# The memory's norm gain moved from its tokens into its weights, in a fused two-block transformer kernel

## The reference

```
def rmsnorm(x, gain):
    y = x32 * lax.rsqrt(jnp.mean(x32 * x32, axis=-1, keepdims=True) + EPS)
    return (y * gain.astype(f32)).astype(x.dtype)
...
    km, vm = jnp.split(mem_n @ w_kv, 2, axis=-1)      # mem_n = rmsnorm(mem, norm_mem)
```

## Time and profile before

| | us |
|---|---|
| median of 3 runs | 756.17 (754.99 to 756.32) |
| the profiled execution, its time | 757.29 |
| its span, first to last instruction | 755.5 |
| TensorE matmuls busy | 737.4 (98%) |
| VectorE busy | 523.7 (69%) |
| ScalarE busy | 472.9 (63%) |
| DMA queue of SyncE | 125.91 MB, 52.2% of 16 engines' span |

### The profile page before, as it was taken

The page is one execution under the profiler, slowest core; times in us unless marked ns, Lnnn a source line. Parts: engine busy times, 40 slices in busy tenths (PEclk is TensorE's granted clock), DMA queues, the critical chain, the costliest instruction groups (busy, mean ns, idle before and its releaser), DMA issues.

```text
span 755.5 us, 10829 instructions
## 1 busy us (share of the span) xinstructions
PE 737.4 (98%) x3887; PEld 612.0 (81%) x3887; DVE 523.7 (69%) x811; ACT 472.9 (63%) x746; POOL 10.9 (1%) x18
## 2 busy tenths in 40 slices
PE   8999999999999999999999999998899999999998
PEld 5778888987898888888888887866679888888886
DVE  5686596676767777767547487999957765567540
ACT  6676648866367778777435776666636776557420
POOL 0004000000000000000000000000000000000000
PEclk9999999999999999999999999999999999999999
DMA  8875465434366665456656356210247755566630
GB/s 280 284 257 171 131 190 187 152 114 147 111 218 205 218 222 183 150 170 208 198 178 191 118 167 196 85 56 29 71 144 235 236 193 175 173 223 212 208 109 28
DMA packets 70986, 128.87 MB, mean 171 GB/s; under 512 B 5575, under 2 KB 17823, under 8 KB 70944
## 3 DMA queue, kind: packets, MB, share of 16 engines
q1 hardware_dynamic: 70366, 125.91, 52.2%
q10 hardware_dynamic: 578, 2.40, 1.0%
HBM read 127.24 MB, written 1.05 MB: 170 GB/s over the span
## 4 chain that ended last, share of the span: by engine, by line
PE 88%; DMA 4%; DVE 4%; ACT 2%; issue 1%; SPq 1%; DVEq 0%; ACTq 0%
PE acc L600 26%; PE acc L602 26%; PE acc L601 26%; DMA b_x<-in_x 1%; PE banks L739 1%; DMA b_raw<-in_w_in 1%; DVE b_wlo L1484 1%; PE banks L651 1%; PE banks L634 1%; PE banks L914 1%; DMA b_gain<-in_norm_ffn 1%; PE banks L621 1%; DMA b_gates<-in_b_gate 1%; PE banks L666 1%; PE banks L780 1%
## 5 line engine op out<-in xcount | busy, mean ns | idle before, releaser
L1484 DVE TENSOR_TENSOR b_wlo<-b_raw,b_whi 128x1024 fp32r<-128x1024 f32 (+3 forms) x244 | 274.3, 1154 | 89.8 <-ACT b_whi L1029 88.4
L1029 ACT ACTIVATE b_whi<-b_raw 128x1024 fp32r<-128x1024 f32 (+3 forms) x244 | 239.2, 1003 | 122.7 <-PE acc L602 45.3
L600 PE MATMUL acc<-b_whi,b_hhi 128*128 128x512 f32 (+4 forms) x528 | 201.8, 382 | 2.6 <-DVE b_wlo L1484 1.1
L602 PE MATMUL acc<-b_wlo,b_hhi 128*128 128x512 f32 (+4 forms) x528 | 196.5, 372 | 0.0
L601 PE MATMUL acc<-b_whi,b_hlo 128*128 128x512 f32 (+4 forms) x528 | 196.3, 372 | 0.0
L600 PEld LDWEIGHTS acc<-b_whi,b_hhi 128*128 128x128 f32 x528 | 99.4, 188 | 22.3 <-issue 2.8
L602 PEld LDWEIGHTS acc<-b_wlo,b_hhi 128*128 128x128 f32 x528 | 99.4, 188 | 15.3
L601 PEld LDWEIGHTS acc<-b_whi,b_hlo 128*128 128x128 f32 x528 | 99.6, 189 | 14.2
L600 PE MATMUL acc<-b_whi,b_ohi 128*128 128x512 f32 (+1 forms) x272 | 105.8, 389 | 0.3 <-DVE b_olo L2030 0.3
L602 PE MATMUL acc<-b_wlo,b_ohi 128*128 128x512 f32 (+1 forms) x272 | 103.6, 381 | 0.0
L601 PE MATMUL acc<-b_whi,b_olo 128*128 128x512 f32 (+1 forms) x272 | 103.5, 380 | 0.0
(11 more groups left out here) (258 smaller groups left out, 748.6 us busy)
## 6 DMA issues: line engine op xcount, KB each, us to landing
b_raw<-in_w_in SPq DMA_DIRECT2D x48, 512.0 KB, 4.3
b_raw<-in_w_ffn_up SPq DMA_DIRECT2D x40, 512.0 KB, 4.8
b_raw<-in_w_ffn_in SPq DMA_DIRECT2D x40, 512.0 KB, 4.6
b_raw<-in_w_ffn_down SPq DMA_DIRECT2D x22, 512.0 KB, 5.8
b_raw<-in_w_ffn_out SPq DMA_DIRECT2D x22, 512.0 KB, 4.5
b_raw<-in_w_out SPq DMA_DIRECT2D x16, 512.0 KB, 3.8
b_raw<-in_w_in SPq DMA_DIRECT2D x12, 412.0 KB, 3.6
b_raw<-in_w_in SPq DMA_DIRECT2D x8, 410.0 KB, 3.6
```

The lines of the kernel that those rows point to most:

```text
L600: nc.tensor.matmul(o, a, wh, start=first, stop=False)
L602: mm = nc.tensor.matmul(o, a, wl, start=False, stop=last)
L1029: A(whi[:, n % SPLIT, 0:c["nk"], 0:c["n"]], raw[:, n % RAW, 0:c["nk"], 0:c["n"]], ACT.Copy)\
L1484: V.tensor_tensor(wlo[:, n % SPLIT, 0:c["nk"], 0:c["n"]], raw[:, n % RAW, 0:c["nk"], 0:c["n"]], whi[:, n % SPLIT, 0:c["nk"], 0:c["n"]].bit ...
```

## The change

The gain is loaded as 8 rows of 128 entries instead of one row of 1024, and one transpose on TensorE makes of it a tile of 128 partitions x 8 columns, copied by ScalarE into `gcol`. The rounded part of the four `mkv` chunks is made with that column as the scale, the rest by a scaled subtract; each chunk takes two instructions on each engine, one for each 128 features, in place of one. The memory's tokens are turned straight from `memx` when they have landed; the four gain multiplies and the spread go. Two more idle matmuls follow the turned gain. SyncE's wait before it overwrites `memx` at group `fg0` is on the four turned banks instead of the gain multiplies. One wait is added ahead of the turn of `iq` in the second block, on a group that was finished long before. VectorE no longer waits for a bank before the gain multiplies of `x1`.

```diff
-ORDER1["dve"] = [("norm gain", "mem", 1, 0), ("norm gain", "mem", 0, 0), ("norm gain", "mem", 0, 1), ("lo", "mkv", 0),
-     ("norm lo", "mem", 0, 0), ("norm gain", "mem", 1, 1), ("lo", "mkv", 1), ("norm lo", "mem", 0, 1),
+ORDER1["dve"] = [("lo", "mkv", 0), ("norm lo", "mem", 0, 0), ("lo", "mkv", 1), ("norm lo", "mem", 0, 1),
...
+        gcol = sb("gcol", [P, KT])
...
-        memg = gates[0:1, 0, D:2 * D]
+        memg = gates[0:KT, 0, D:D + P]
...
+                src = memx if k == "mem" else xn
...
-                    pe.wait_ge(*at("tokens scaled", f"{k} {t} {b}"))
+                    pe.wait_ge(*((sem(f"mem {t} in"), 16) if k == "mem" else at("tokens scaled", f"{k} {t} {b}")))
...
-            def spread(k, row):
-
-                pe.wait_ge(sem(f"{k} gain row in"), 16)
-                for b in range(2):
-                    mm = nc.tensor.matmul(acc[1][b][:, :], ones[0:1, 0:P], row[:, b * CN:(b + 1) * CN], start=True, stop=True)
-                mm.then_inc(sem(f"{k} gain spread"), 1)
+            def gain_column():
+
+                pe.wait_ge(sem("mem gain row in"), 16)
+                nc.tensor.transpose(acc[1][0][:, 0:KT], memg, ident[0:KT, 0:KT]).then_inc(sem("mem gain turned"), 1)
...
             idle(2)
-            spread("mem", memg)
             pe.wait_ge(sem("identity in"), 16)
+            gain_column()
+            idle(2)
...
+                if name == "iq":
+                    pe.wait_ge(*moved("iqb", 1))
...
-                            sp.wait_ge(*at("tokens scaled", "mem 1 1"))
+                            for bank in range(2 * T):
+                                sp.wait_ge(*at(f"bank{bank} full", "memT"))
...
-            act.dma_start(memg, dram["norm_mem_2"]).then_inc(sem("mem gain row in"), 16)
+            act.dma_start(memg, dram["norm_mem_2"][0, :].rearrange("(k p) -> k p", p=P)).then_inc(sem("mem gain row in"), 16)
...
+                if c["w"] == "w_mem_kv_2":
+                    for k in range(c["nk"]):
+                        ins = A(whi[:, n % SPLIT, k, 0:c["n"]], raw[:, n % RAW, k, 0:c["n"]], ACT.Copy,
+                                scale=gcol[:, c["row"] // P + k:c["row"] // P + k + 1])
...
+            act.wait_ge(sem("mem gain turned"), 1)
+            done(A(gcol[:, :], acc[1][0][:, 0:KT], ACT.Copy), "mem gain column", "0")
+            act.wait_ge(*at("mem gain column", "0"))
...
+                if c["w"] == "w_mem_kv_2":
+                    for k in range(c["nk"]):
+                        ins = V.scalar_tensor_tensor(wlo[:, n % SPLIT, k, 0:c["n"]], raw[:, n % RAW, k, 0:c["n"]],
+                                                     gcol[:, c["row"] // P + k:c["row"] // P + k + 1],
+                                                     whi[:, n % SPLIT, k, 0:c["n"]].bitcast(F32), ALU.mult, ALU.subtract)
...
-                elif kind == "norm gain" and k == "mem":
-                    c, t = rest
-                    norm_gain(k, memx, None, c, t, [(sem("mem gain spread"), 1), (sem(f"mem {t} in"), 16)])
...
-                    norm_gain(k, x, gain, c, t, [gain_at(1), (sem(f"x {t} in"), 16), at(f"bank{2 * t + c} full", "memT")])
+                    norm_gain(k, x, gain, c, t, [gain_at(1), (sem(f"x {t} in"), 16)])
```

More of the change, by code:

```diff
@@ L621, in norm_T @@
                         mm = nc.tensor.transpose(X[2 * t + b][:, c * P:(c + 1) * P],
-                                                 xn[:, t, (4 * b + c) * P:(4 * b + c + 1) * P], ident)
+                                                 src[:, t, (4 * b + c) * P:(4 * b + c + 1) * P], ident)
                     full(mm, 2 * t + b, f"{k}T")
@@ L1028, in hi_one @@
                     act.wait_ge(sem("chunk used"), n - SPLIT + 1 + PER * i)
-                A(whi[:, n % SPLIT, 0:c["nk"], 0:c["n"]], raw[:, n % RAW, 0:c["nk"], 0:c["n"]], ACT.Copy)\
-                    .then_inc(sem("hi ready"), 1)
+                if c["w"] == "w_mem_kv_2":
+                    for k in range(c["nk"]):
+                        ins = A(whi[:, n % SPLIT, k, 0:c["n"]], raw[:, n % RAW, k, 0:c["n"]], ACT.Copy,
+                                scale=gcol[:, c["row"] // P + k:c["row"] // P + k + 1])
+                else:
+                    ins = A(whi[:, n % SPLIT, 0:c["nk"], 0:c["n"]], raw[:, n % RAW, 0:c["nk"], 0:c["n"]], ACT.Copy)
+                ins.then_inc(sem("hi ready"), 1)
             def hi_to(n):
@@ L1483, in lo_one @@
                 dve.wait_ge(sem("hi ready"), n + 1 + PER * i)
-                V.tensor_tensor(wlo[:, n % SPLIT, 0:c["nk"], 0:c["n"]], raw[:, n % RAW, 0:c["nk"], 0:c["n"]],
-                                whi[:, n % SPLIT, 0:c["nk"], 0:c["n"]].bitcast(F32), ALU.subtract)\
-                    .then_inc(sem("lo ready"), 1)
+                if c["w"] == "w_mem_kv_2":
[3 more added lines that the diff above has]
+                                                     whi[:, n % SPLIT, k, 0:c["n"]].bitcast(F32), ALU.mult, ALU.subtract)
+                else:
+                    ins = V.tensor_tensor(wlo[:, n % SPLIT, 0:c["nk"], 0:c["n"]], raw[:, n % RAW, 0:c["nk"], 0:c["n"]],
+                                          whi[:, n % SPLIT, 0:c["nk"], 0:c["n"]].bitcast(F32), ALU.subtract)
+                ins.then_inc(sem("lo ready"), 1)
             def lo_to(n):
@@ L1509, in norm_gain @@
                 h = slice(b * CN, (b + 1) * CN)
-                done(V.tensor_tensor(xn[:, t, h], src[:, t, h], g[:, h] if k != "mem" else acc[1][b][:, :],
-                                     ALU.mult), "tokens scaled", f"{k} {t} {b}")
+                done(V.tensor_tensor(xn[:, t, h], src[:, t, h], g[:, h], ALU.mult), "tokens scaled", f"{k} {t} {b}")
             def norm_lo(k, hi, lo, b, tiles=range(T)):
```

## The result

The changed kernel takes 758.36 us (median of 7 runs, 757.51 to 760.57) against 756.17 us for the kernel before (7 runs, 754.90 to 758.41); the ratio is 1.0036, 95% interval 1.0024 to 1.0048. It is slower by some 2.2 to 2.7 us, where no change was forecast.

A forecast was written before the change was run, and what follows sets the result against it. TensorE was taken as the bound, its unbroken run from about 28 us starting when chunk 4 lands. Profiled 757.29 us, 0.0 from the front, 0.0 to +0.1 behind, median 1.12 lower: 756.1 us, no change, range 754.5 to 757.7.

The forecast's parts named there:

- the sum: Whole kernel: profiled 757.29 us, 0.0 from the front, 0.0 to +0.1 behind; median 1.12 below, so 756.1 us.
- that unbroken run: TensorE from about 28 us: no gap to give; one matmul wait of 0.3 us up to 440 us.
- the clock's rival: Before the first `qa` matmul: the longer wait lowers the clock, 1.2 to 1.7 us lost, 757.4 to 757.9; chance 0.09.
- Chunk 4: Load of `w_in` at the start: ScalarE takes it at 23.0 as before, first `qa` matmul again at 25.4.
- The transpose and the copy of the gain: Head of the kernel: 0.5 us for both, hidden behind the transfer of ScalarE's first chunk.
- Two scaled pieces: Each `mkv` chunk: ScalarE 0.2 us more than 1.06, at most 1.36; VectorE 0.15 more than 1.22, at most 1.49.
- The first product matmul: Start of the memory's product: 9.8 to 10.7 against 10.67, so up to 0.9 us won there.
- The second memory tile: Ahead of the memory's turns: landed by 8.08, so TensorE's added wait for it ends by 8.1.
- the turn of `x1`: TensorE, before 16.82: arrives up to 0.7 us earlier, tokens ready and first turn at 16.2 to 16.6.
- The memory's product: TensorE at the start: ends at 23.7 at the best, 24.4 if the late chunk pushes it, both before 25.37.
- the wait ahead of `qa`: First `qa` matmul: its wait for a weight's rest grows from 1.1 to between 1.1 and 1.7 us.
- Chunk 7: Weight load: issued 0.3 us later, at worst 0.6, landing at 27.9 to 28.2; ScalarE takes it at 28.29, free.

The follow-up runs named there:

- e1: Changed kernel with the gain column's tile `gcol` 16 columns wide instead of 8, no instruction different; 755.26 us, ratio 0.9992 to the kernel before.
- e2: Kernel before with an unused tile of 8 columns (32 bytes) behind the last common tile; 758.35 us, ratio 1.0030.
- e4: Kernel before with 32 bytes put in front of `ahi`, moving only the feed-forwards' tiles; 757.93 us, ratio 1.0025.
- e6: Kernel before with the four tiles of turned tokens 32 bytes further; its filler also put `ahi` at 192 modulo 256; 767.05 us, ratio 1.0147.
- e3: Kernel before with an unused tile of 16 columns (64 bytes) behind the last common tile; 755.09 us, ratio 0.9997.
- e14: e3 with two idle matmuls added behind the spread of the gain, nothing else of the change; 756.47 us, ratio 1.0003 to the kernel before.
- e12: e1 without the two idle matmuls that the change added; 754.94 us, ratio 0.9984 to the kernel before.
- e5: Kernel before with the split weights 32 bytes further; fillers also put the turned tokens at 0 and `ahi` at 192 modulo 256; 768.17 us, ratio 1.0162.

## Why the prediction was wrong

**The step that failed** is none of the terms of the sum but one that the sum lacked. The forecast went through the change part by part and counted instructions, waits and transfers; the tile that it declares was not counted at all. Its 32 bytes cost 2.3 us, in 528 matmuls of which no line had changed and which lie from 344 us on. The sentence "the change, whose work lies wholly in the first 24 us, can only move the instant from which that unbroken run starts" was wrong in just this: the run's own pace was taken as given. (Nor is that run unbroken: the earlier trace rows end at 440 us, and between there and 600 the matmuls of the kernel before wait some dozen times, once for 2.2 us.) In place of the forecast's 0.0 the runs show a step of 229.3 ns become 233.7 in the last 240 of these matmuls, and the loss gone when the tile is made 64 bytes (e1). The range's upper end, 757.7, had been set by the clock's rival, and that rival did not occur: the changed kernel's granted clock from 24 to 29 us is 1.00. (The sum itself, 757.29 - 1.12, gives 756.17 and not 756.1; nothing hangs on it.)

```profile
24.00:29.00 5.00, 3.98 (x16) 2.66 (x16) 4.76 (x6) 4.71 (x9) 0.00 (x0) 1.00 0.78 249
```

**The start, point by point.** Chunk 4 at 23.0 and the first `qa` matmul at 25.4 held. The transpose and the copy of the gain took 0.5 us in all (5.02 to 5.51), as taken. Two scaled pieces took 1.33 us on ScalarE (1.26 taken, 1.36 the bound) and 1.41 on VectorE (1.37 taken, 1.49 the bound). The first product matmul at 9.90 was forecast at "near 9.8". The second memory tile held the turns up until 8.38, where 8.1 was taken. VectorE was later than its bounds allowed: its first multiply of `x1` began at 16.18, where 15.48 to 15.9 was forecast, so the turn of `x1`, forecast at 16.2 to 16.6, came at 16.92. The memory's product ended at 25.40 - 0.73 = 24.67, outside the forecast's 23.7 to 24.4 and 0.4 later than before, though it had begun 0.8 earlier; and the wait ahead of `qa` shrank to 0.73 us where it should have grown to 1.1 to 1.7. Chunk 7 was issued at 18.93, right behind the scaled rest of chunk 3 (17.49 + 1.42 = 18.91), which is 0.7 later than before and beyond the 0.6 taken for the worst. It landed at 26.9 all the same, earlier than the 27.6 of before, because the transfer took 8.0 us and not 9.4: here the forecast was saved by luck.

```profile
17.49 1.42 DVE L1497 SCALAR_TENSOR_TENSOR b_wlo<-b_raw,b_gcol,b_whi 128x512 fp32r<-128x512 f32 x2
```

```profile
L1005 SPq DMA_DIRECT2D b_raw<-in_w_in x1: 541/541/541, 18.9 to 18.9; - x1
...
DMA to landing us min/median/max: 8.0/8.0/8.0
```

**One execution was read as the kernel.** The forecast took the start to be bound by the landing of chunk 4. That was true of the profiled execution and of three others among the eleven (e2, e4, e6); in the other seven the product itself was the bound. That the start would bring nothing came out right (e1 against e3), but in part by luck: for the seven the reason given does not hold, and what evens the start out later was seen in e3 and e14 alone. And the two late falls of the clock in that execution hid the loss when the spans were compared.

**The clock at the start.** With the added idle matmuls the granted clock was 1.00 from 7 to 12 us, against 0.66 before; without them (e12) it was 0.71 there and 0.51 from 12 to 16 us, and the time was no longer, 754.94 us against e1's 755.26. The Trainium skill's "TensorE: Matmul & The Clock Gate", section What's actually happening, has the slow clock as the default that activity lifts; the rows of 7 to 12 us agree. The lift can come late: in e12 the clock stayed at its lower level from 12 us to 15.9 with TensorE busy all the time. The changed kernel's window, then e12's:

```profile
7.00:12.00 5.00, 3.85 (x23) 2.77 (x21) 3.08 (x5) 4.37 (x9) 0.00 (x0) 1.00 1.05 398
```

```profile
7.00:12.00 5.00, 3.24 (x13) 2.64 (x14) 3.37 (x5) 4.62 (x9) 0.00 (x0) 0.71 1.06 388
...
12.00:16.00 4.00, 4.00 (x13) 3.13 (x13) 2.79 (x6) 3.04 (x7) 0.00 (x0) 0.51 0.91 325
```

## What to carry to other kernels

Count a declared tile as part of a change: where tiles follow one another in memory, even an unused one moves all behind it. When TensorE bounds a kernel and its spacing differs between two builds of the same instructions, compare where the stationary and the moving operand start modulo 256, and try them at the same place. Keep fillers to multiples of 256 where the other tiles are to stay; those of e5 and e6 were not, and moved what they should have held. Follow one instruction through both traces before trusting two spans: over a stretch of 240 matmuls without waits, the seven executions at distance 0 agree to a tenth of a nanosecond a step.

## What the hardware showed that was not expected

With float32r operands, 128 x 128 stationary and 512 columns moving, the spacing of back-to-back matmuls is 227.1 ns when both operands start at the same byte modulo 256, 229.3 at a distance of -64, 232.7 at 128, 233.7 at -32, 32 and 64, and 234.1 at 96, with weight loads of the same 188 ns. When all products are off distance 0, this kernel loses 12.3 us (e5) or 11.2 us (e6). The two kernels named "before" and "after" here both lie off the best place. A filler that brings the distance to 0 takes either to some 755 us: for the changed kernel that is 3 us gained (e1), for the kernel before 0.5 us, less than its runs can tell from nothing (e3).
